# Sums of the w_mod units one block later, and in the PEER stage 12 gathered rows of u early and a quarter of the one-hots on ScalarE

## The reference, cut to what matters

```python
mod_x = (jax.nn.silu(c) @ w_mod[l] + b_mod[l])[:, None, :]
sh1, sc1, g1, sh2, sc2, g2 = jnp.split(mod_x, 6, axis=-1)
...
px = hx @ w_in[l] + b_in[l]
...
def _peer(h, wq, keys, u, v):
    q = (hf @ wq).reshape(T, PEER_HEADS, 2, PEER_HALF)
    s = jnp.einsum('thpd,hpkd->thpk', q, keys)
    s1, i1 = lax.top_k(s[:, :, 0], PEER_TOPK)
    s2, i2 = lax.top_k(s[:, :, 1], PEER_TOPK)
    ...
    top_s, pos = lax.top_k(cand_s, PEER_TOPK)
    idx = jnp.take_along_axis(cand_i, pos, axis=-1)
    w = jax.nn.softmax(top_s, axis=-1)
    ...
        a = jnp.einsum('td,thkd->thk', hb, u[ib])
        coef = (wb * jax.nn.gelu(a, approximate=False)).astype(v.dtype)
        return jnp.einsum('thk,thkd->td', coef, v[ib])
```

## Time and profile before

| what | value |
|---|---|
| median of 3 runs | 4639.11 us (4627.49 to 4652.63) |
| profiled execution, its own time | 4631.02 us |
| its span | 4629.4 us, 56578 instructions |
| granted TensorE clock, mean over the span | 0.957 |
| busy: TensorE / VectorE / ScalarE / GpSimd | 4217.7 (91%) / 2940.6 (64%) / 1336.3 (29%) / 1270.9 us (27%) |
| TensorE's loads of weights | 3625.9 us (78%) |
| data moved | 917.43 MB, mean 198 GB/s |
| chain of waits that ended last | TensorE 63%, VectorE 14%, DMA 11%, issue 7%, ScalarE 4% |

### The profile page before, as it was taken

How to read it: one execution, slowest core, us unless ns; L and a number is a source line. 1 busy time by engine, 2 the same in 40 slices (tenths; PEclk the granted TensorE clock), 3 DMA queues, 4 the chain that set the end, 5 groups by cost and what they waited for, 6 DMA issues and landing times.

```text
span 4629.4 us, 56578 instructions
## 1 busy us (share of the span) xinstructions
PE 4217.7 (91%) x21035; PEld 3625.9 (78%) x21035; DVE 2940.6 (64%) x3379; ACT 1336.3 (29%) x1429; POOL 1270.9 (27%) x643
## 2 busy tenths in 40 slices
PE   7899999999979979598999999699997999999996
PEld 2588777788867868477999998699996888888885
DVE  0333656555536643555799998577775777777776
ACT  0322332344431122222233444122222222222221
POOL 0001333000002310133556443577772122211110
PEclk9899999999989989799999999899998999999998
DMA  8325666100015663176455568999996888888883
GB/s 291 106 75 150 189 187 175 52 32 32 34 41 155 190 164 100 62 173 147 119 142 145 138 169 200 319 360 362 361 363 233 318 329 319 315 317 312 315 304 131
DMA packets 698201, 917.43 MB, mean 198 GB/s; under 512 B 135467, under 2 KB 533859, under 8 KB 661987
## 3 DMA queue, kind: packets, MB, share of 16 engines
q1 hardware_dynamic: 620147, 562.95, 39.8%
q0 software_dynamic: 40928, 285.23, 16.6%
q10 hardware_dynamic: 37008, 67.65, 4.9%
HBM read 846.51 MB, written 69.22 MB: 198 GB/s over the span
## 4 chain that ended last, share of the span: by engine, by line
PE 63%; DVE 14%; DMA 11%; issue 7%; ACT 4%; POOL 1%; SPq 1%; DVEq 0%; ACTq 0%; POOLq 0%
PE ps L117 19%; PE ps L118 19%; PE ps L119 19%; DMA pu<-in_peer_u_dram 8%; DVE oneJ L1739 3%; DVE pT L1646 2%; PE ps L1922 2%; DMA wm<-in_w_mod_dram 1%; DVE mred L1334 1%; DVE ring L1761 1%; PE ps L2081 1%; ACT wh L820 1%; DVE oneI L1740 1%; DVE tk_pick L1714 0%; ACT L830 0%
## 5 line engine op out<-in xcount | busy, mean ns | idle before, releaser
L117 PE MATMUL ps<-h2h,pTuh 128*128 128x384 f32 x2048 | 708.6, 346 | 89.8 <-POOL pTul L744 88.7
L744 POOL TENSOR_TENSOR pTul<-pT,pTuh 128x1024 fp32r<-128x1024 f32 x256 | 650.8, 2543 | 505.6 <-ACT pTuh L1101 503.4
L119 PE MATMUL ps<-h2h,pTul 128*128 128x384 f32 x2048 | 695.1, 339 | 0.0
L118 PE MATMUL ps<-h2l,pTuh 128*128 128x384 f32 x2048 | 694.7, 339 | 0.0
L117 PE MATMUL ps<-vDh,coh 128*128 128x512 f32 x1536 | 601.9, 392 | 28.8 <-DVE col L1457 28.8
L118 PE MATMUL ps<-vDl,coh 128*128 128x512 f32 x1536 | 601.3, 391 | 0.0
L119 PE MATMUL ps<-vDh,col 128*128 128x512 f32 x1536 | 600.7, 391 | 0.0
L1101 ACT ACTIVATE pTuh<-pT 128x1024 fp32r<-128x1024 f32 x256 | 271.9, 1062 | 841.9 <-DVE pT L1646 834.7
L720 POOL TENSOR_TENSOR mbuf<-mbuf,silu 128x2048 f32<-128x2048 f32 x64 | 257.9, 4029 | 924.1 <-DMA mbuf<-in_w_mod_dram 923.4
L117 PEld LDWEIGHTS ps<-h2h,pTuh 128*128 128x128 f32 x2048 | 392.7, 192 | 104.0 <-POOL pTul L744 89.1
L1646 DVE STREAM_TRANSPOSE pT<-pu 128x1024 f32<-128x1024 f32 x256 | 317.3, 1241 | 223.8 <-DMA pu<-in_peer_u_dram 166.1
(11 more groups left out here) (334 smaller groups left out, 7820.2 us busy)
## 6 DMA issues: line engine op xcount, KB each, us to landing
vraw<-in_peer_v_dram SPq DMA_DIRECT2D x128, 1024.0 KB, 6.9
mbuf<-in_w_mod_dram SPq DMA_DIRECT2D x64, 1024.0 KB, 5.9
pu<-in_peer_u_dram ACTq DMA_DIRECT2D x256, 256.0 KB
pu<-in_peer_u_dram SPq DMA_DIRECT2D x256, 256.0 KB
wraw<-in_w_in_dram SPq DMA_DIRECT2D x48, 1024.0 KB, 8.6
wm<-in_w_mod_dram SPq DMA_DIRECT2D x16, 2048.0 KB, 8.7
gelu_scratch<-act_g SPq DMA_DIRECT2D x128, 192.0 KB
route_scratch<-route SPq DMA_DIRECT2D x24, 1024.0 KB, 5.8
```

The costliest lines, as they stand in the source:

```text
L117: pe.matmul(out, lh, rh, start=first, stop=False)
L118: pe.matmul(out, lh, rl, start=False, stop=False)
L119: return pe.matmul(out, ll, rh, start=False, stop=last)
L744: pool.tensor_tensor(pTul[s][:, c, :], pT[s][:, c, :], pTuh[s][:, c, :].bitcast(fp32), ALU.subtract).then_inc(u_lo, 1)
```

## The change

There are three parts. Lines with - are of the kernel before, lines with + of the kernel after.

**Sums.** The sum of unit j comes after block 18 + j instead of block 17 + j, in bank 6 instead of bank 4 (bank 4 is the first one that the attention uses); the last one stands behind the first rope product, and the biases are added behind the first queries.

```diff
-            with pe.Fori(0, 16) as i:
-                px_block(2 * i + 17, 1)
-                mod_sum(2 * i, 0, 4, 4 * i)
+            px_block(17, 1)
+            with pe.Fori(0, 15) as i:
                 px_block(2 * i + 18, 0)
-                mod_sum(2 * i + 1, 1, 4, 4 * i + 2)
+                mod_sum(2 * i, 0, 6, 4 * i)
+                px_block(2 * i + 19, 1)
+                mod_sum(2 * i + 1, 1, 6, 4 * i + 2)
+            px_block(48, 0)
+            mod_sum(30, 0, 6, 60)
...
             rope_part(0)
+            mod_sum(31, 1, 6, 62)
             pe.wait_ge(w_out_, NPX)
...
             mod_reduce(31, 1, 1)
-            mod_finish(0, 2 * DC, 4)
...
             queries(0)
+            mod_finish(0, 2 * DC, 6)
             attention_pair(0)
```

```diff
+EARLY_AT = (2, 4, 6, 8)
+EARLY = len(EARLY_AT) * DB
+LEFT = SLOTS - EARLY
...
+        ring_e = [sb(f"ring_e{k}", 64 + 8 * k, [P, D]) for k in range(2)]
...
-            return min(3 * n, 2 * n + 4)
+            return EARLY + min(3 * n, (LEFT - 3) * n // (NK - LATE - 2) + 3)
...
+            def gather_early(k):
+                if k >= 2:
+                    pool.wait_ge(ring_used, k - 1)
+                pool.indirect_dma_start(ring_e[k % 2][:, :], None, u_rows, bass.IndirectOffsetOnAxis(
+                    ap=sidx[:, k:k + 1], axis=0)).then_inc(ring_in[k % 2], 16)
...
-            with pool.Fori(0, LATE // 2 + 1) as i:
+            with pool.Fori(0, TK // 2) as i:
                 for s in range(2):
                     for h in range(2):
                         u_low(2 * i + s, s, h)
-            pool.wait_ge(tk_chosen, 2)
-            for ss in r_stored:
-                pool.wait_ge(ss, 64 * (TD // RT // 2) + 16)
+            pool.wait_ge(sc_set, 2 * PH)
+            for i in range(TK, P0):
+                u_low(i, i % 2, 0)
+                if i == TK + 1:
+                    pool.wait_ge(tk_chosen, 2)
+                if i % TK in EARLY_AT:
+                    gather_early(len(EARLY_AT) * (i // TK - 1) + EARLY_AT.index(i % TK))
+                u_low(i, i % 2, 1)
+            with pool.Fori(P0 // 2, LATE // 2 + 1) as i:
+                for s in range(2):
+                    for h in range(2):
+                        u_low(2 * i + s, s, h)
+            pool.wait_ge(r_stored[0], 64 * (TD // RT // 2) + 16)
             for i in range(LATE + 2, NK):
                 for k in range(rows_before(i), rows_before(i) + 1):
+                    if k == EARLY + 3:
+                        pool.wait_ge(r_stored[1], 64 * (TD // RT // 2) + 16)
                     gather_u(k)
...
+            def dot_early(k):
+                dve.wait_ge(ring_in[k % 2], 16 * (k // 2) + 16)
+                dve.scalar_tensor_tensor(out=ring_e[k % 2][:, :], in0=ring_e[k % 2][:, :], scalar=1.0, in1=h2tok,
+                                         op0=ALU.mult, op1=ALU.mult, accum_out=dots[:, k:k + 1]).then_inc(ring_used, 1)
...
                 def turn(n):
                     u_turn(i + (n + 3) // 2, (n + 3) // 2 % 2, (n + 3) % 2)
+                    if b > 0 and n in (5, 9, 13, 17):
+                        dot_early(len(EARLY_AT) * (b - 1) + (5, 9, 13, 17).index(n))
```

```diff
+            def one_j(n):
+                g = 4 * n + 3
+                act.wait_ge(r_done, g - 1)
+                if not isinstance(n, int) or n >= 1:
+                    act.wait_ge(oneJ_set, n)
+                for t in range(4):
+                    ins = act.activation(absd[:, t, :], iota[:, :], ACT.Abs, bias=chT[:, 1, bass.ds(4 * g + t, 1)], scale=-1.0)
+                ins.then_inc(oneJ_abs, 1)
+                act.wait_ge(oneJ_abs, n + 1)
+                for t in range(4):
+                    at = bass.ds(4 * g + t, 1)
+                    ins = act.activation(oneJ[1][:, t, :], absd[:, t, :], ACT.Relu, bias=chT[:, 2, at], scale=nchw[:, at])
+                ins.then_inc(oneJ_set, 1)
...
                         keep_route(32 * r + 4 * k + q, 6 + q % 2, slot, 4 * (k % 4) + q)
+                        if q == 1:
+                            one_j(8 * r + k)
...
-                for t in range(4):
+                for t in range(4 if both else 0):
...
-                one_hots(g + 3, 1)
+                one_hots(g + 3, 1, both=False)
...
-            def routing(g, s):
+            def routing(g, s, made):
                 pe.wait_ge(one_set, g + 1)
+                if made is not None:
+                    pe.wait_ge(oneJ_set, made + 1)
```

More of the change, by code:

```diff
@@ L256, in layer_kernel @@
         dots, scoef = sb("dots", 206, [P, SLOTS]), sb("scoef", 206.5, [P, SLOTS])
+        absd = sb("absd", 200, [P, 4, P])
+        nchw = sb("nchw", 94, [P, TD])
         oneJ = [sb(f"oneJ{s}", 40 + 2 * s, [P, 4, P]) for s in range(2)]
@@ L344, in layer_kernel @@
             sem(n) for n in ("tk_chain", "iota_in", "tk_diff", "tk_exp", "tk_chosen", "ch_turned", "ch_set"))
-        one_set, r_done, r_set = sem("one_set"), sem("r_done"), sem("r_set")
+        one_set, oneJ_abs, oneJ_set, r_done, r_set = (sem(n) for n in ("one_set", "oneJ_abs", "oneJ_set", "r_done", "r_set"))
         r_stored = [sem(f"r_stored{s}") for s in range(2)]
@@ L748, in _ @@
             v_rows = a["peer_v"][0]
+            def gather_early(k):
[3 more added lines that the diff above has]
+                    ap=sidx[:, k:k + 1], axis=0)).then_inc(ring_in[k % 2], 16)
             def gather_u(k):
[L751 removed]
+                n = k - EARLY
+                if n >= 4:
                     pool.wait_ge(ring_used, k - 3)
[L753 to L754 removed]
+                pool.indirect_dma_start(ring[n % 4][:, :], None, u_rows, bass.IndirectOffsetOnAxis(
+                    ap=sidx[:, k:k + 1], axis=0)).then_inc(ring_in[n % 4], 16)
             def gather_v(k):
+                n = LEFT + k
                 pool.wait_ge(ring_used, SLOTS + k - 3)
[L758 to L761 removed]
+                pool.indirect_dma_start(ring[n % 4][:, :], None, v_rows, bass.IndirectOffsetOnAxis(
+                    ap=sidx[:, k:k + 1], axis=0)).then_inc(ring_in[n % 4], 16)
+            with pool.Fori(0, TK // 2) as i:
                 for s in range(2):
@@ L1155, in route_part @@
                         keep_route(32 * r + 4 * k + q, 6 + q % 2, slot, 4 * (k % 4) + q)
-            with act.Fori(0, TD // RT // 2) as r:
+                        if q == 1:
+                            one_j(8 * r + k)
+            route_part(0)
+            with act.Fori(1, TD // RT // 2) as r:
                 route_part(r)
@@ L1727, in _ @@
             dve.tensor_copy(sw[:, :], chosen[:, 2, :]).then_inc(tk_chosen, 1)
-            with dve.Fori(0, DB) as b:
+            dve.wait_ge(h2_turned, DC + 4)
+            for b in range(DB):
                 top_experts(b + 1, TK * b + TK)
@@ L1731, in _, with one_hots @@
                 dve.wait_ge(ch_turned, b + 1)
-                dve.tensor_copy(chT[:, :, bass.ts(b, P)], pb[7][:, 0:3 * P].rearrange("p (w t) -> p w t", w=3)).then_inc(ch_set, 1)
-            def one_hots(g, s):
+                dve.tensor_copy(chT[:, :, bass.ts(b, P)], pb[7][:, 0:3 * P].rearrange("p (w t) -> p w t", w=3))
+                dve.tensor_scalar(nchw[:, bass.ts(b, P)], pb[7][:, 2 * P:3 * P], -1.0, None, ALU.mult).then_inc(ch_set, 1)
+            def one_hots(g, s, both=True):
                 if not isinstance(g, int) or g >= 2:
                     dve.wait_ge(r_done, g - 1)
-                for t in range(4):
+                for t in range(4 if both else 0):
                     at = bass.ds(4 * g + t, 1)
@@ L1756, in _, with ring_count @@
                     route_block(2 * r + P0 + s, s, 8 * r + 4 * s)
+            def ring_count(n):
+                return 16 * (n // 4) + 16 + (8 * EARLY if n % 4 < 2 else 0)
             def dot(k):
-                dve.wait_ge(ring_in[k % 4], 16 * (k // 4) + 16)
-                dve.scalar_tensor_tensor(out=ring[k % 4][:, :], in0=ring[k % 4][:, :], scalar=1.0, in1=h2tok, op0=ALU.mult, op1=ALU.mult,
-                                         accum_out=dots[:, k:k + 1]).then_inc(ring_used, 1)
-            dve.wait_ge(h2_turned, DC + 4)
+                n = k - EARLY
+                dve.wait_ge(ring_in[n % 4], ring_count(n))
+                dve.scalar_tensor_tensor(out=ring[n % 4][:, :], in0=ring[n % 4][:, :], scalar=1.0, in1=h2tok, op0=ALU.mult,
+                                         op1=ALU.mult, accum_out=dots[:, k:k + 1]).then_inc(ring_used, 1)
             for i in range(LATE, NK):
@@ L1776, in axpy @@
             def axpy(k):
-                at = SLOTS + k
-                g, t = ring[k % 4][:, :], acc[:, 0, :]
-                dve.wait_ge(ring_in[k % 4], 16 * (at // 4) + 16)
+                at = LEFT + k
+                g, t = ring[at % 4][:, :], acc[:, 0, :]
+                dve.wait_ge(ring_in[at % 4], ring_count(at))
                 if k == 0:
@@ L1782, in axpy @@
                 else:
-                    dve.wait_ge(ring_used, at)
+                    dve.wait_ge(ring_used, SLOTS + k)
```

(2 more changed lines are left out.)

5 lines of the change are left out of this document (removed).

## The result

The kernel after takes 4578.6 us (median of 4 runs, 4571.8 to 4584.5) against 4638.4 us (4 runs, 4627.5 to 4652.6): ratio 0.987, 95% interval 0.986 to 0.989. Its profiled execution took 4577.7 us, span 4576.0. The forecast was 4572 us, so 7 us too low, and the three parts have to be looked at one by one, since errors of both signs can lie in a sum.

The account below looks back on a forecast made before the run. Bounds were taken by stage: waiting sums in the input products, TensorE and VectorE in the top-k, VectorE in routing, DMA bytes late. -47 - 4 - 16 = -67 us from 4639 gave 4572 us, range 4540 to 4605.

Parts of the forecast that it names:

- Part A: Input products: sums moved one block later no longer wait for their reduction, 31 blocks of 11.13 us, -47 us.
- rivals 1 and 6: Input products: 1, feed loop takes the sum's place, 4589 us, 13%; 6, TensorE's wait only moves, 4619 us, 3%.
- Part B, the price: Top-k: 12 early dots of 2.25 us on VectorE plus slower clock, +29 us, bounds +10 and +38.
- rivals 4 and 5: Top-k: 4, dots mostly covered (cost 10), 4553 us, 10%; 5, early dots wait for late gathers, 4728 us, 2%.
- GpSimd's issues cost nothing: Top-k: GpSimd's gather issues and buffer waits are free; at most 1 us each, 12 us, if splits have no slack.
- Part B, the gain: Late stage, taken as bound by bytes: 12 fewer gathered rows at 362 GB/s, -33 us, bounds -18 and -40.
- room, but little: Late stage: TensorE's own block takes at most 8.6 us, against 8.7 us for the bytes with the rows gone.
- the outer bound of 40: Late stage: what GpSimd's earlier start of the gathers may bring lies only in the -40 us bound.
- 33 us shorter at the same 362 GB/s: Late stage: sign that the forecast is right, 33 us less time at an unchanged byte rate.
- Rival 3: Late stage gives back only 15 of 33 us as TensorE's 8.6 us a block bind: 4590 us, 9%.
- Part C: Routing: a quarter of the one-hots moved to ScalarE, blocks from 12.9 to 12.1 us, -16 us, bounds 0 and -21.
- at most -21: Routing: TensorE's own limit, routings 2.97 us apart, 282.5 us against 303.5 for all 96.

Follow-up runs that it names:

- e4_nodots: The kernel after with its 12 early dot products left out, the rows still gathered: 4560.7 us, top-k stretch 380.8 us.
- e7_onerow: The kernel after with one late row a block, 62 in place of 116, the other 54 rows left out: 4522.5 us.
- e2_early: The kernel before with part B alone (12 early rows, 116 late ones, the new pacing rule): 4640.3 us beside 4640.65 us.
- e5: The kernel after without early rows (128 late rows), keeping the earlier start of the late gathers: 4563.1 us beside 4638.1 before, ratio 0.984.
- e12: As e5, with ScalarE's one-hots in a third buffer, issued behind the block's first route copy: 4564.9 us beside 4640.0 before, ratio 0.985.

## Why the prediction was right, and where it was not

**Part A** (-47, measured -48.3). Right in size and way: no sum of line 2056 waits in the input products, they stand 11.13 us apart as forecast, the stretch between first and last sum is a full TensorE at clock 1.00, and rivals 1 and 6 are out: TensorE never waits for wl there.

**Part B, the price** (+29, measured +24.8). Here the phases of 96 to 98 us, the 8 us wait for the chosen experts (I had said 10) and the slower clock (0.95 in the two phases) came as forecast; rivals 4 and 5 are out. "GpSimd's issues cost nothing" was wrong in its ground: e4_nodots shows 8.7 us that come with the gathers alone, inside the 12 us that I had kept as a bound.

**Part B, the gain** (-33, measured -18.2; -21.5 over eleven kernels). The forecast of the whole held, but this term of it failed. I priced a row by its bytes at 362 GB/s and named TensorE's 8.6 us a block as a limit with "room, but little". e7_onerow puts that limit at 8.26, and still a row brought a third of its bytes' time in the blocks, and more, 2 to 2.5 us, only in the opening. The 12 rows together gave 13 to 16 us; the rest came from the new rule for the order of the rows, to which the prediction gave no term, and the earlier start, to which it gave only the outer bound of 40. The rate fell from 362 to 343 GB/s: the test that I had set, "33 us shorter at the same 362 GB/s", failed on both counts. Rival 3 (15 of 33) had the size nearly right, for the rows alone quite right, and the place (TensorE's own block) right in part. Taken together part B cost +24.8 - 18.2 = +6.6 us in this pair, where I had -4; alone (e2_early) it moved the time by nothing that can be told. A version that keeps the new rule and the earlier start and drops the early rows (e5, e12) is likely the better one.

**Part C** (-16, measured -14.5). The number came by another way, so it was right by luck. I had VectorE bound at 12.1 us a block with its oneI behind GpSimd's split. In the trace oneI comes first and the split waits, VectorE has 51 us to spare, and TensorE sets the pace: I had listed that limit (at most -21, from 2.97 us between routings) and taken it for the far bound. Seven of the first eight blocks run at it, and the 12.1 us and more of the others are this limit and a late load at each fourth routing. The page "ScalarE: Activation LUTs" of the Trainium skill puts relu-like work on VectorE (Rules for kernel authors), from which I had drawn that part C would bring nothing; measured it brings 14 to 15 us, with VectorE full and ScalarE half idle before. The same page has abs and relu in every table set (Table sets: the hidden batching unit), and the trace agrees: no load of a table stands in the routing stage.

**The sum.** Against the forecast the span lost 1.3 us more in A and 4.2 more in B's price, and 14.8 less in B's gain, 1.5 less in C and 2.8 around the marks: 13.6 us in all, -53.4 for -67. Between the medians the change is 59.8 us (4638.4 to 4578.6), so that 7 us remain of the 13.6; the rest is how the two profiled executions lie in their runs. That the whole came out within 7 us is in part luck too: part B's late stage missed by 15 us, and A and B's price, both better than forecast, gave 5.5 of it back.

## What to carry to other kernels

Before a gain is priced by bytes, measure the same stage with most of the bytes gone: here the next limit (8.26 us a block) lay 10% under the present pace (9.2), and a row taken away gave a third of its share. Count as a change of its own what only seems to serve another one: the new rule for the order of the rows, with the earlier start, was worth more than half as much as the rows. Work moved here from one full stage to another was paid in full where it arrived (2 us a row) and refunded in part where it left; the two have to be measured apart. And a stage that spreads by 5 us between runs can't be read to 5 us from one pair of profiles: take it over every run that leaves it alone. An engine that is busy 99.8% of a stretch can still be late once a block: compare its steps with those of a stretch where nothing holds it.

## What the runs showed of the hardware

The busy share of the DMA engines is no measure of how full they are. The queues of e7_onerow from 2900 to 3350, and of the kernel before from 2990 to 3490 (packets, MB, share of 16 engines):

```profile
q0 software_dynamic: 7715, 56.25, 36.9%
q1 hardware_dynamic: 23955, 41.05, 31.3%
q10 hardware_dynamic: 15269, 27.79, 24.9%
```

```profile
q0 software_dynamic: 15783, 114.99, 62.7%
q1 hardware_dynamic: 23040, 38.41, 23.6%
q10 hardware_dynamic: 15264, 27.79, 16.7%
```

The same 27.79 MB on q10 took 24.9% of 450 us in the one and 16.7% of 500 us in the other, 112 against 84 us, with half the gathers beside them. The share was 0.93 at 278 GB/s, in a stretch where TensorE is busy 441.8 of 450 us, and 1.03 at 362. I had taken the 1.03 for a sign that the stage is bound by its bytes.

Which of two engines yields when VectorE and GpSimd meet depends on who is running: two oneI in a row held GpSimd's split up (3.28 us for 2.40), two splits in a row went with one long tk_pick (6.57 us for 2.5 to 3.2). That the one holds the other up is read from their times; no run here moves one of these instructions by itself.
